# Modulation products of a two-block transformer: three buffers and other places for their loads, and five products moved into the first feed-forward

## What is computed

```python
for l in range(DEPTH_2):
    shift, scale, gate = jnp.split((silu_c @ w_mod[l] + b_mod[l])[:, None, :], 3, axis=-1)
    shift_c, scale_c, gate_c = jnp.split(silu_cc @ w_mod[l] + b_mod[l], 3, axis=-1)
    h = modulate(x, g_pre[l], shift, scale)
    hc = modulate(ctx, g_pre[l], shift_c, scale_c)
    ...
```

## Time and profile before

| | us |
|---|---|
| median of 3 runs | 1717.1 (1715.94 to 1718.62) |
| profiled execution | 1714.67 |
| its span, first to last instruction | 1712.9 |
| PE busy (matmul) | 1555.7 |
| DVE busy | 939.0 |
| ACT busy | 729.8 |

### The profile page before, as it was taken

The page is one execution under the profiler, slowest core; times in us unless marked ns, Lnnn a source line. Parts: engine busy times, 40 slices in busy tenths (PEclk is TensorE's granted clock), DMA queues, the critical chain, the costliest instruction groups (busy, mean ns, idle before and its releaser), DMA issues.

```text
span 1712.9 us, 25830 instructions
## 1 busy us (share of the span) xinstructions
PE 1555.7 (91%) x9958; PEld 1360.4 (79%) x9958; DVE 939.0 (55%) x1481; ACT 729.8 (43%) x1245; POOL 121.5 (7%) x145
## 2 busy tenths in 40 slices
PE   6999998889999889868898898999997998988996
PEld 6999997679999867656677777888774887878996
DVE  5777776537777568565533335233326446435554
ACT  5444562554444454225433253222325355435443
POOL 3700000130000130001000000000000011010000
PEclk9999998999999999989999999999998999989999
DMA  8655543246777433431111122333320332314662
GB/s 288 213 184 182 179 161 107 92 144 227 241 236 246 161 123 123 148 123 37 37 62 62 50 74 74 99 111 111 110 75 25 119 106 71 111 51 146 202 205 99
DMA packets 72662, 223.22 MB, mean 130 GB/s; under 512 B 6656, under 2 KB 23552, under 8 KB 71936
## 3 DMA queue, kind: packets, MB, share of 16 engines
q1 hardware_dynamic: 54528, 195.20, 34.7%
q10 hardware_dynamic: 18048, 26.82, 4.8%
HBM read 220.94 MB, written 1.05 MB: 130 GB/s over the span
## 4 chain that ended last, share of the span: by engine, by line
PE 80%; DVE 8%; ACT 6%; DMA 4%; issue 2%; POOL 0%; SPq 0%; DVEq 0%; ACTq 0%
PE ps L476 68%; DMA ring<-stream 3%; PE ps L486 2%; DVE w_lo L415 1%; PE ps L891 1%; ACT w_hi L1084 1%; ACT area L1333 1%; PE ps L932 1%; PE ps L949 1%; PE ps L875 1%; DVE area L2094 1%; PE ps L912 1%; DVE area L1914 1%; DVE area L1523 1%; PE ps L831 1%
## 5 line engine op out<-in xcount | busy, mean ns | idle before, releaser
L476 PE MATMUL ps<-hn_hi,w_hi 128*128 128x256 f32 (+1 forms) x1888 | 616.4, 326 | 59.8 <-DVE w_lo L415 33.9
L476 PE MATMUL ps<-hn_lo,w_hi 128*128 128x256 f32 (+1 forms) x1888 | 605.9, 321 | 0.0
L476 PE MATMUL ps<-hn_hi,w_lo 128*128 128x256 f32 (+1 forms) x1888 | 605.4, 321 | 0.0
L415 DVE TENSOR_TENSOR w_lo<-ring,w_hi 128x1024 fp32r<-128x1024 f32 (+1 forms) x331 | 395.5, 1200 | 359.5 <-ACT w_hi L1084 355.4
L1084 ACT ACTIVATE w_hi<-ring 128x1024 fp32r<-128x1024 f32 (+1 forms) x347 | 359.6, 1037 | 350.8 <-DMA ring<-stream 241.9
L476 PEld LDWEIGHTS ps<-hn_hi,w_hi 128*128 128x128 f32 x1888 | 366.6, 194 | 93.0 <-DVE w_lo L415 37.0
L476 PEld LDWEIGHTS ps<-hn_lo,w_hi 128*128 128x128 f32 x1888 | 366.7, 194 | 24.2
L476 PEld LDWEIGHTS ps<-hn_hi,w_lo 128*128 128x128 f32 x1888 | 365.9, 194 | 24.9
L1147 ACT ACTIVATE area<-ps 128x512 f32<-128x512 f32 (+1 forms) x164 | 80.8, 503 | 348.1 <-PE ps L476 337.0
L476 PE MATMUL ps<-area_r,w_hi 128*128 128x256 f32 (+1 forms) x512 | 117.7, 324 | 2.0 <-DVE w_lo L415 1.9
L476 PE MATMUL ps<-hid_hi,w_hi 128*128 128x256 f32 x352 | 99.4, 282 | 2.4 <-DVE w_lo L415 1.2
(11 more groups left out here) (295 smaller groups left out, 1665.1 us busy)
## 6 DMA issues: line engine op xcount, KB each, us to landing
ring<-stream SPq DMA_DIRECT2D x359, 512.0 KB, 3.6
mod_at<-mod_stream ACTq DMA_DIRECT2D x29, 512.0 KB, 5.4
area<-mod_stream ACTq DMA_DIRECT2D x17, 512.0 KB, 4.1
pk<-pack ACTq DMA_DIRECT2D x1, 1610.0 KB, 7.0
pk<-pack SPq DMA_DIRECT2D x1, 1549.0 KB, 12.4
h<-x_in SPq DMA_DIRECT2D x1, 1024.0 KB, 5.0
cond_at<-cond SPq DMA_DIRECT2D x2, 512.0 KB, 14.4
mod_at<-mod_stream SPq DMA_DIRECT2D x2, 512.0 KB, 12.6
```

The lines of the kernel that those rows point to most:

```text
L415: eng.tensor_tensor(lo[:, 0:w], raw, hi[:, 0:w].bitcast(F32), ALU.subtract).then_inc(lo_ready[who], 1)
L476: m = pe.matmul(dst, w_, x_, start=(start and n == 0), stop=(stop and n == 2), skip_group_check=True)
```

## The change

Three edits. The late products get three buffers in place of two, with semaphores of their own (`late_loaded0` to `2`), and load m waits for product m - 3. Loads 36 to 38 are issued as the stage begins; each further one is issued by ACT within `high_part`, behind the high part of the unit behind whose low part DVE has that product (dq2 for 39, up to dg2 for 47). And five products, 5 to 9, are done in the first feed-forward, at f = 8, 11, 14, 17 and 20, behind the power tables' part, with loads issued at f = 6, 9, 12, 15 and 18 (for 6 to 10; load 5 stays at f = 4); ACT's loop there is written out. All later numbers move on by five: the projections have 10 to 13, the second feed-forward 14 to 35, and 12 remain late (36 to 47), none of them behind dg3. ACT waits for all 48 products ahead of rk0.

```diff
@@ -40,7 +40,8 @@
 NEG = -1e30
 LAYERS = 2
 MODS = LAYERS * 3 * KT
-EARLY_MODS = 5
+EARLY_AT = [0, 1, 2, 3, 4, 8, 11, 14, 17, 20]
+EARLY_MODS = len(EARLY_AT)
 FFN_MODS = [0, EARLY_MODS + 4]
 LATE_MOD = FFN_MODS[1] + FT
 LAM_INIT = [0.8 - 0.6 * float(np.exp(-0.3 * l)) for l in range(LAYERS)]
@@ -323,7 +324,7 @@
         assert Area.at <= AREA, Area.at
         o_dif, o_ret, o_mlp = diffz[:, 8:12, :], retz[:, 8:12, :], mlpu[:, 0:4, :]
         as_mod = lambda v: quarter(v.rearrange("p a b -> p (a b)"))
-        late_mod_slot = lambda m: as_mod(retz[:, 8 + 2 * (m % 2):10 + 2 * (m % 2), :])
+        late_mod_slot = lambda m: as_mod(retz[:, 6 + 2 * (m % 3):8 + 2 * (m % 3), :])
         late_cond = lambda st: as_mod(retv[:, 2 * st:2 * st + 2, :])
 
         def rounded(at):
@@ -418,8 +419,13 @@
 
             if not first:
                 eng.wait_ge(s("mod_used"), m - 1 + body)
-            slot = mod_slot(m) if m < LATE_MOD else late_mod_slot(m)
-            eng.dma_start(slot, mod_stream[m + body]).then_inc(s(f"mod_loaded{m % 2}"), 16)
+            eng.dma_start(mod_slot(m), mod_stream[m + body]).then_inc(s(f"mod_loaded{m % 2}"), 16)
+
+        def load_late_mod(eng, m):
+
+            if m >= LATE_MOD + 3:
+                eng.wait_ge(s("mod_used"), m - 2)
+            eng.dma_start(late_mod_slot(m), mod_stream[m]).then_inc(s(f"late_loaded{m % 3}"), 16)
 
         DT, LRE, LIM, R, K, GC, GS, COS, SIN, PR, QI, DEN, CR, CI, TMP, LR = range(16)
         G4, R4 = 22, 0
@@ -1083,6 +1089,9 @@
                 w = UNIT_WIDTH(name)
                 act.activation(w_parts(name)[0][:, 0:w], ring[:, u % RING, 0:w], ACT.Copy).then_inc(hi_ready, 1)
                 done[0] = n + 1
+                late = u - UNIT["dk", 0, 3] + LATE_MOD
+                if LATE_MOD + 3 <= late < MODS:
+                    load_late_mod(act, late)
 
             def high_parts(count):
 
@@ -1114,28 +1123,30 @@
                     load_mod(act, m0 + 1)
                 part(4)
                 gated_high(0, FT * n + 1)
-                lead = 8 * (1 - n)
-                for f in range(1, 1 + lead):
-                    part(3 * f + 2)
-                    gate(f, UNIT[tag, "w3", f] + 1)
-                    part(3 * f + 3)
-                    gated_high(f, FT * n + f + 1)
-                    if f < EARLY_MODS:
-                        load_mod(act, m0 + f + 1)
-                    part(3 * f + 4)
-                    if f == 4:
-
-                        act.wait_ge(s("angle_ready"), 1)
-                        act.activation(s5v[:, 7:9, :], s5v[:, 5:7, :], ACT.Sin, scale=TWO_PI).then_inc(s("angle_sin"), 1)
-                with act.Fori(0, (FT - 2 - lead) // 4) as it:
-                    for f in range(1 + lead, 5 + lead):
-                        part(3 * f + 2, 12 * it)
-                        gate(f, UNIT[tag, "w3", f] + 1 + 12 * it)
-                        part(3 * f + 3, 12 * it)
-                        gated_high(f, FT * n + f + 1 + 4 * it)
-                        if n == 1:
+                if n == 0:
+                    for f in range(1, FT - 1):
+                        part(3 * f + 2)
+                        gate(f, UNIT[tag, "w3", f] + 1)
+                        part(3 * f + 3)
+                        gated_high(f, f + 1)
+                        if f <= 4:
+                            load_mod(act, f + 1)
+                        elif f % 3 == 0:
+                            load_mod(act, f // 3 + 4)
+                        part(3 * f + 4)
+                        if f == 4:
+
+                            act.wait_ge(s("angle_ready"), 1)
+                            act.activation(s5v[:, 7:9, :], s5v[:, 5:7, :], ACT.Sin, scale=TWO_PI).then_inc(s("angle_sin"), 1)
+                else:
+                    with act.Fori(0, (FT - 2) // 4) as it:
+                        for f in range(1, 5):
+                            part(3 * f + 2, 12 * it)
+                            gate(f, UNIT[tag, "w3", f] + 1 + 12 * it)
+                            part(3 * f + 3, 12 * it)
+                            gated_high(f, FT * n + f + 1 + 4 * it)
                             load_mod(act, m0 + f + 1, 4 * it)
-                        part(3 * f + 4, 12 * it)
+                            part(3 * f + 4, 12 * it)
                 part(FU - 1)
                 gate(FT - 1, UNIT[tag, "w3", FT - 1] + 1)
                 gated_high(FT - 1, FT * n + FT)
@@ -1313,15 +1324,8 @@
 
 
             act.wait_ge(block2_loaded, 32)
-            load_mod(act, LATE_MOD)
-            load_mod(act, LATE_MOD + 1)
-            late = [LATE_MOD + 2]
-
-            def next_mod(l):
-
-                if l == 0 and late[0] < MODS:
-                    load_mod(act, late[0])
-                    late[0] += 1
+            for m in range(LATE_MOD, LATE_MOD + 3):
+                load_late_mod(act, m)
 
             def diff(l, step):
                 nd = len(DIFF[l])
@@ -1422,22 +1426,18 @@
                     for j in range(4):
                         t_ = 2 * T if part == "dk" else tok
                         take((part, l, j), diffz[:, (0 if part == "dk" else 4) + j, 0:t_], tokens=t_)
-                        if (part, j) > ("dk", 1):
-                            next_mod(l)
                 for tt in range(4):
                     take(("dv", l, tt), diffv[:, tt, :], tokens=BW, unit=("dv", l, 3))
-                    next_mod(l)
                 for j in range(4):
                     take(("dg", l, j), diffz[:, 8 + j, 0:tok], ACT.Silu, tokens=tok)
-                    next_mod(l)
-                while l == 0 and late[0] < MODS:
-                    next_mod(l)
                 root_table()
                 if l == 0:
                     act.wait_ge(s("lay_dve"), 3)
                 for slot, name in enumerate(slot_units(l)):
                     prepare(name)
                     part, j = name[0], name[2]
+                    if l == 0 and slot == 0:
+                        act.wait_ge(s("mod_used"), MODS)
                     if part == "rk":
                         take(name, retz[:, j, 0:2 * T], tokens=2 * T)
                     if part == "rq":
@@ -1529,7 +1529,10 @@
 
             def modulation(m, body=0):
 
-                dve.wait_ge(s(f"mod_loaded{m % 2}"), 16 * (m // 2 + 1) + 8 * body)
+                if m < LATE_MOD:
+                    dve.wait_ge(s(f"mod_loaded{m % 2}"), 16 * (m // 2 + 1) + 8 * body)
+                else:
+                    dve.wait_ge(s(f"late_loaded{m % 3}"), 16 * ((m - LATE_MOD) // 3 + 1))
                 if m == 0:
                     dve.wait_ge(cs_ready, 2)
                 else:
@@ -1652,12 +1655,12 @@
                         gated(f, f + 1)
                         part(3 * f + 3)
                         gated_low(f, f + 1)
-                        if f < EARLY_MODS:
-                            modulation(f)
-                        elif f < EARLY_MODS + 2:
-                            turn_tables(f - EARLY_MODS)
-                        else:
-                            input_powers(f - EARLY_MODS - 2)
+                        if 5 <= f < 7:
+                            turn_tables(f - 5)
+                        if f >= 7:
+                            input_powers(f - 7)
+                        if f in EARLY_AT:
+                            modulation(EARLY_AT.index(f))
                         part(3 * f + 4)
                 else:
                     with dve.Fori(0, (FT - 2) // 4) as it:
```

## The result

| | before | after |
|---|---|---|
| median, us | 1717.81 (1715.94 to 1718.62, 4 runs) | 1701.45 (1698.46 to 1703.61, 4 runs) |
| profiled execution, us | 1714.67 | 1701.44 |
| its span, us | 1712.9 | 1699.7 |

The ratio is 0.9905, with a 95% interval of 0.9887 to 0.9923: 16.4 us less. The forecast was 20.2 us less, 1696.9; the measured time lies 4.5 us above it and inside the range of 1692 to 1705.

What follows compares the result with a forecast made beforehand. PE, busy 91%, was held in the late stage by the load and product queue, not work. 22.4 + 1.9 - 0.4 - 2.9 - 0.85 = 20.2 us off the 1717.1 median gave 1696.9, range 1692 to 1705.

Steps and rivals of the forecast that it cites:

- (b): Scores and rk1 behind rk0: low clock at 767, blamed on the long stall, goes; gain 1.9 us, bounds 0 and 3.0.
- (d): First feed-forward: five added products delay w2's low part, so PE waits 0.45 to 0.7 us each; cost 2.9 us, bounds 0 and 12.
- (e): First feed-forward: five added loads slow ring loads, priced 0.17 each from the second feed-forward; cost 0.85 us, bounds 0 and 3.5.
- (a): Late-product stage: no late low part, PE runs dg0 to rk0 without a stop; gain 22.4 us in idle time and low clock.
- the clock stays down: Rival, late stage: PE idles no more but low-clock stretches come anyway, so 2.9, 2.1 and 1.9 aren't gained; 1703.8 us, chance 0.09.
- (c): Start of the late stage: a third load issued ahead of the second block's squares; cost 0.4 us, bounds 0 and 0.45.
- rival of the colliding loads: First feed-forward: ring loads beside modulation loads land in twice 3.5 us, costing 8.0 for 0.85; 1704.1 us, chance 0.04.
- slower rival: Late stage: ACT holds high parts for loads waiting on products, 8.8 us per unit, nine units lose 30 us; 1727, chance 0.03.

Runs made afterwards that it cites:

- run 7: Changed kernel with the five products still moved, but the 12 late products as before (two buffers, loads behind the evictions): 1707.55 us, ratio 0.9952 to the kernel before.
- run 10: Changed kernel with all 17 products late, none moved, six buffers, and layer 0's diff-branch attention steps one unit later: 1692.45 us, ratio 0.9865 to the kernel before.
- run 8: Changed kernel with the five moved products behind w2's low part instead of ahead, repeated beside the changed kernel: 1695.44 us, ratio 0.9883 to the kernel before.
- run 9: Changed kernel with all 17 products late, six buffers, and the first three late loads behind the second block's squares: 1692.18 us, ratio 0.9860 to the kernel before.
- run 2: Changed kernel with loads 6 to 10 cut to 32 KB, products whole: 1700.16 us, ratio 0.9920 to the kernel before.
- run 1: Changed kernel with the five moved products made on 64 of 1024 columns, loads whole: 1695.97 us, ratio 0.9893 to the kernel before.
- run 5: The changed kernel again, unaltered, as base of the second job: 1702.03 us, ratio 0.9920 to the kernel before.
- run 4: Changed kernel with the five moved products behind w2's low part instead of ahead, first job: 1697.01 us, ratio 0.9897 to the kernel before.
- run 3: Changed kernel with the five moved products on 64 columns and, of loads 6 to 10, only load 7 whole: 1695.68 us, one run.

## Why the prediction was right, and where it was off

The forecast of 20.2 us less for the profiled execution (1694.5) met 1701.44, 6.9 us above; the median lies only 4.5 above its forecast, since 2.4 us had been added there for the distance of the profiled execution from the median of before. Of the terms (b) is off by 3.2 us, (d) by 1.3 and (e) by 2.4, which makes up the 6.9. That the time still fell inside the range is in part the width of the range: no single rival was what happened. By its steps:

**(a) Late products: right to 0.1 us** (22.35 for 22.4). All that it named is there: no late low part, products 4 to 6 us behind their high parts, no hold of ACT, and run 7 shows that the two stalls have different causes. The loads in the second half of the stage land in 4.0 to 5.9 us where 4.1 was taken; the reserve took it up, of which 5 us were left at the least (dg2's low part), where 6 were forecast.

**(b) The low clock at 767: wrong.** The step that failed is "I take the stall for its cause". The full clock ahead of it had come back, and it fell all the same, for 3.4 us in the first step and 6.8 in the second: 1.3 us lost for 1.9 gained. Run 10 shows a fall behind the 1.78 us gap alone, with no stall for over 30 us. The gap was in the earlier trace rows and its bound of 0 in the text; even that was too kind, since rk2, at the full clock before, now has the low one. The size of this loss is not the change's alone: run 8 has the same code from dg0 on, its clock does not fall in the second step, and from the first scores behind rk0 to those behind rk2 it takes 27.9 us, where it is 28.4 before and 29.8 in the changed kernel. Why the fall takes one form or the other is open. The rival "the clock stays down" had the mechanism, but not for the stretches at 720 and 756, which did go.

**(c) The third load: right.** 0.42 us for 0.4, and run 9 shows that it is this issue, with two hidden beside DVE's tile. It reaches PE: from the root ahead of the squares to dk0's first matmul it is 13.38 us in the changed kernel and 12.97 in run 7, which has two issues and the low clock in the same place. Against the trace of before it can't be seen (14.48), since there a stretch of clock 0.50 lies in the sum of squares.

**(d) Five products: the mechanism was right, the term too small**, 4.2 us for 2.9 (run 2). The low part of w2 follows the product, as worked out, and PE turned to it at 100.43 in the trace of before, as taken. But at f = 8 PE went on at 101.12, 0.17 us behind the 100.95 at which the low part was to be ready, and a wait costs another 0.10 us of overlap behind it.

**(e) Five loads: the term that failed most**, 3.2 us for 0.85. The price of 0.17 came from the second feed-forward, where DVE has one product and no tables: reserve covers a late ring there, as it does in run 1, where the same loads cost 0. In the iterations of the change the product had already spent the reserve, so a delay of 0.8 us goes through to PE one for one (a wait costs 0.6 to 1.1 us with the ring at 3.5, 1.6 to 1.8 with the ring late, in runs 2, 5 and 7 and the changed kernel). The two terms were priced apart and added; they share one reserve. It is near the upper bound, 5 x 0.7 = 3.5 us with no reserve at all. The reason given, that an iteration with a product never has a load behind f = 7, didn't help, since the ring stays late for iterations after the load. The rival of the colliding loads had the right resource, but the landing of the ring load beside ACT's did not double to 7.0: it became 4.5 to 4.9 us in the changed kernel, and 6.1 at the most (run 4). That the queues share the engines, as the Trainium skill says ("DMA: Bandwidth & Descriptors", "Queues, rings and completion order"), the trace bears out; what its turn-taking doesn't give is a delay with one queue empty.

Of the slower rival nothing came: ACT waits for no product in the stage.

## What to carry to other kernels

A late load can lie in the queue that issues it, not in the memory: look at what the issuing engine waits for just ahead (here evictions that all wait for one unit), and put the issue behind something that runs early. When two small costs fall into the same iteration, subtract both from the one reserve before pricing either; and work that is put ahead of something that PE is about to need costs what the same work behind it does not (6.6 us between the medians of runs 5 and 8, 6.4 by their traces, for one product moved past one low part). If a clock stretch is to be counted as a gain, look for any other gap near it that could bring the clock down anyway.

## What was unexpected of the hardware

A ring load of 512 KB lands in 3.5 us alone and in 4.2 to 4.6 after one load on ACT's queue, although that has landed by then: for two or three loads in run 3, for one, two or nine in run 5, for eight and more in the changed kernel and nearly all through the feed-forward in run 1. The data's volume matters: with 32 KB on ACT's queue it stays at 3.5 (run 2). Why it lasts, and why it differs between equal loads, is not settled.

The granted clock fell to 0.50 for 6.8 us behind a single idle gap of 1.78 us, after 32.7 us of matmuls without a pause at 1.00 (run 10). There it fell 0.5 us behind the gap's end (745.75); in the changed kernel, with 27.2 us ahead of the same gap, 2.5 us behind it (751.15), in another gap of 0.74 us, and for 3.4 us at first. The length of the work ahead doesn't order the two forms: the kernel before had 7.5 us ahead and run 7 30.3, and both fell right behind the gap. What decides between them was not tested.
